# A fused decoder block on eight cores: three weight loads issued later, zero columns written once, the last 128 tokens in narrower column groups

## The chip, the cores and the metric

The program runs on the 8 cores of one Trainium2 chip. Each core works on one of the 8 sequences of the batch, with the same weights, and the cores do not exchange data. The metric is the time of one execution in microseconds of the device, taken on the slowest of the eight cores. "Before" is the kernel as it stood, "after" is the changed one.

## The reference

Each core computes one decoder block for a sequence of 2048 tokens with 1024 channels:

```
z = x @ w_in                                  # q, k, v | pool input | gates
y_attn = moba_attention(q, k, v) @ w_branch_attn
y_pool = multiscale_pool(u_pool) @ w_branch_pool
mix = (g_attn * y_attn + g_pool * y_pool) @ w_out
x = layer_norm(ALPHA * x + mix, ln1_g, ln1_b)
a = x @ w_ffn_gate                            # (2048, 2816)
u = x @ w_ffn_up
ap = pad(a, two zero tokens in front)
a = sum(ap[:, i:i + s] * conv_w[i] for i in range(3)) + conv_b
ffn = (gelu(a) * u) @ w_ffn_down
x = layer_norm(ALPHA * x + ffn, ln2_g, ln2_b)
```

The change touches three places: the gated merge (`mix`) with the loads around it, the two zero tokens ahead of the causal convolution, and the last product with the layer norm behind it.

## The kernel before, in words

The tokens are worked on in two halves of 1024. All tiles are placed by hand in one SBUF arena, and a small scheduler in the kernel (`Sched`) records every operation in program order, finds the overlaps of what is read and written, and puts a semaphore wait ahead of an operation where another engine, a DMA or an earlier operation of the same engine has to be done. Each engine runs its operations in the order in which they were recorded. The order on TensorE is made by `weave`, which takes pieces of generators (`Stream`) in turn by a virtual time; a load that a generator records between two of its `yield`s doesn't change that order.

There are two DMA queues. `ld_cast` (L407) issues loads on GpSimd's queue (POOL in the profile) that cast float32 in HBM to bf16 in SBUF: all weights. `ld`, `ld_x1` and the output writes are issued on SP's queue.

The stages, in order: projections and attention woven together; `merge(0)` at the end of that; then `merge(1)` woven with `oproj(0)` (output projection, first layer norm, transposes into `x1T`); then `p7_gen(0)` (gate and up products, convolution, GELU) woven with `oproj(1)`; then `p7_gen(0)` alone, `p8(0)` (down product and second layer norm), `p7_gen(1)`, `p8(1)`.

The merge of one half runs over 8 column blocks j. A block uses one of three buffers `wm` (L407, 768 KB of bf16 each), and behind a block `mg_load` issues the load of the block three further on into the buffer that has come free. The load that is issued behind block j = 0 of the second half is thus needed at block j = 3. `wout`, 2048 KB, is issued when the first weave is through, just ahead of the second half's merge, and `p7_load` three times right behind it: it loads the gate/up weights `wgu` of one f (a block of 128 of the 2816 channels, 512 KB) into one of three buffers. `p7_gen` uses one buffer for each f and issues the load of f + 3 behind it.

In `p7_gen` the gate product of 1024 tokens goes into `abuf[f % 2]`, a float32 row of two columns ahead of 1024. In the first half the two columns are zero (a memset on VectorE, L453), in the second half they are the last two columns of the first half, kept in `halo`.

In `p8` a tile of 128 tokens has two PSUM banks of 512 columns. For each, 22 matmuls of 128 x 512 are followed by a scalar_tensor_tensor that adds the residual (L449) and a bn_stats (L1120); then come bn_aggr (L1122), an addition of EPS (L441), a square root on ScalarE (L433), a reciprocal (L462), and for each half of the columns two scalar_tensor_tensor and a DMA to `out` (L1130). For the last tile all of that stands behind the last matmul of the program.

Of the kernel before, what the change touches and what calls it, by code (L numbers as in the profile page):

```python
# [6 lines left out]
F32 = mybir.dt.float32  # L7
BF16 = mybir.dt.bfloat16
U8 = mybir.dt.uint8
AF = mybir.ActivationFunctionType  # L10
# [8 lines left out]
NF = 22  # L19
# [251 lines left out]
def build_program():  # L271
# [32 lines left out]
    def T(name, shape, dt, off):  # L304
        n = 2 if dt == BF16 else 4
        for d in shape[1:]:
            n *= d
        assert off + n <= ARENA, name
        h = nc.alloc_sbuf_tensor_at(name, list(shape), dt, offset=abase + off)
        S.reg(h, "sb", abase + off, 256 * KB)  # L310
        return h
# [15 lines left out]
    mhalf = T("mhalf", [128, 1], F32, o); o += 32  # L327
    rs = T("rs", [128, 16], F32, o); o += 64
    ps0 = T("psc0", [128, 1], F32, o); o += 32
    assert o <= 4 * KB, o  # L330
    rcw = small[:, 0:16]
    bgate = small[:, 16:32]
# [52 lines left out]
    gbuf = [T(f"gbuf{i}", [128, 512], F32, 174 * KB + 8256 + (2 + i) * 2 * KB) for i in range(2)]  # L385
    assert 174 * KB + 8256 + 8 * KB <= 194 * KB
    wgu = [T(f"wgu{i}", [128, 2, 8, 128], BF16, (194 + 4 * i) * KB) for i in range(3)]

    ps = []
    for i in range(8):  # L390
# [15 lines left out]
    def ld_cast(dst, src, after=()):  # L406
        S.dma("pool", lambda e: e.dma_start(out=dst, in_=src), reads=list(after), writes=[dst])  # L407
# [44 lines left out]
    def memset(eng, ap, val):  # L452
        S.op(eng, lambda e: e.memset(ap, val), writes=[ap])  # L453
# [63 lines left out]
    ld_cast(kh[64:72, :, :], oh8)  # L517
    ld_cast(tri[:], tri_d)
    ld_cast(identb[:], ident_d)
    memset("dve", uh[:], 0.0)  # L520
    memset("pool", mhalf[:], -0.5)
    act(rs[:, 0:1], uh[:, 0, 0:1], AF.Copy)
# [372 lines left out]
    def mg_load():  # L895
        k = mg_n[0]
        mg_n[0] += 1
        if k < 16:
            ld_cast(wm[k % 3][:], wm_d[k % 8])

    def merge(half):
        ui = 0
        for j in range(8):
            w = (half * 8 + j) % 3
            for tl in range(2):
                x_ = xc[half * 2 + tl]
                cs = slice(tl * 512, (tl + 1) * 512)
                s = ui % 2
                ui += 1
                b2 = nbank()  # L910
                for dt in range(8):
                    mm(b2[:, :], wm[w][:, dt, :], x_[:, dt, :], dt == 0, dt == 7)
                    if dt % 4 == 3:
                        yield 4
                act(sga[s][:, :], b2[:, :], AF.Tanh, bias=hb[:, j:j + 1], scale=0.5)
                tile_end()
                b3 = nbank()
                for dt in range(8):
                    mm(b3[:, :], wm[w][:, 8 + dt, :], x_[:, dt, :], dt == 0, dt == 7)
                    if dt % 4 == 3:  # L920
                        yield 4
                act(sgp[s][:, :], b3[:, :], AF.Tanh, bias=hb[:, 8 + j:9 + j], scale=0.5)
                tile_end()
                b0 = nbank()
                for ct in range(4):
                    mm(b0[:, :], wm[w][:, 16 + ct, :], ATT[half][:, ct, cs], ct == 0, ct == 3)
                yield 4
                stt("dve", m1[s][:, :], sga[s][:, :], 1.0, b0[:, :], ALU.add, ALU.mult)
                b1 = nbank()
                for g in range(4):  # L930
                    mm(b1[:, :], wm[w][:, 20 + g, :], PL[half][:, g, cs], g == 0, g == 3)
                yield 4
                stt("dve", m2[s][:, :], sgp[s][:, :], 1.0, b1[:, :], ALU.add, ALU.mult)
                tt("pool", mix[half][:, j, cs], m1[s][:, :], m2[s][:, :], ALU.add)
            mg_load()


    def o_mm(T_):
# [92 lines left out]
    def p7_gen(half, xT):  # L1031
        ui = 0
        pend_tail = []

        def flush_tail():
            while pend_tail:
                s_, f_, cs_, bu_ = pend_tail.pop(0)
                act(gbuf[s_][:, :], cbuf[s_][:, :], AF.Gelu)
                tt("dve", hT[:, f_, cs_], gbuf[s_][:, :], bu_[:, :], ALU.mult)

        for f in range(NF):
            ab = abuf[f % 2]
            if half == 0:
                memset("dve", ab[:, 0:2], 0.0)
            else:
                cp("dve", ab[:, 0:2], halo[:, f, :])
            for c in range(2):
                cs = slice(c * 512, (c + 1) * 512)
                ba, bu = nbank(), nbank()
                w = wgu[(half * NF + f) % 3]  # L1050
                for k, bk in ((0, ba), (1, bu)):
                    for dt in range(8):
                        mm(bk[:, :], w[:, k, dt, :], xT[:, dt, cs], dt == 0, dt == 7)
                        if dt % 4 == 3:
                            yield 4
                s = ui % 2
                ui += 1
                act(ab[:, 2 + c * 512:2 + (c + 1) * 512], ba[:, :], AF.Copy)
                act(cbuf[s][:, :], ba[:, :], AF.Identity, bias=convb[:, f:f + 1], scale=convw[:, f, 2:3])
                stt("dve", cbuf[s][:, :], ab[:, 1 + c * 512:1 + (c + 1) * 512], convw[:, f, 1:2], cbuf[s][:, :], ALU.mult, ALU.add)  # L1060
                stt("dve", cbuf[s][:, :], ab[:, c * 512:(c + 1) * 512], convw[:, f, 0:1], cbuf[s][:, :], ALU.mult, ALU.add)
                flush_tail()
                pend_tail.append((s, f, cs, bu))
            if half == 0:
                cp("dve", halo[:, f, :], ab[:, 1024:1026])
            if half == 1 or f < NF - 3:
                p7_load()
            if half == 0 and f % 2 == 0 and f < 12:
                ld_cast(wd[0][:, f:min(f + 2, 11), :], wd_d[:, f:min(f + 2, 11), :])
            if half == 0 and not O1.live:  # L1070
                wd_late(1)
        flush_tail()
# [10 lines left out]
    def ld_x1(t_):  # L1083
        rw = row[t_ % 4]
        S.dma("sp", lambda e: e.dma_start(out=rw[:, :], in_=x1_d[t_ * 128:(t_ + 1) * 128, :]),
              reads=[("x1", t_)], writes=[rw[:, :]])

    def p8(half):
        banks = {}

        def dmm(tl, bk, hv, f):
            mm(bk[:, :], hT[:, f, tl * 128:(tl + 1) * 128], wd[f // 11][:, f % 11, hv * 512:(hv + 1) * 512], f == 0, f == NF - 1)

        for tl in range(8):
# [10 lines left out]
            if tl == 0:  # L1105
                n0 = 3 if half == 0 else 1
                for t2 in range(1, n0):
                    banks[t2] = [nbank(), nbank()]
                mid = 11 if half == 0 else NF - 1
                for t2 in range(n0):  # L1110
                    for hv in range(2):
                        for f in range(mid):
                            dmm(t2, (bks if t2 == 0 else banks[t2])[hv], hv, f)
            first = (11 if half == 0 else (NF - 1 if tl == 0 else 0)) if tl < (3 if half == 0 else 1) else 0
            for hv in range(2):
                for f in range(first, NF):
# [24 lines left out]
    ld(ln1b[:], lnp_d[1])  # L1141
    M1 = Stream(merge(1))
    O0 = Stream(oproj(0, 1.35), 120.0)
    for _ in range(3):
        p7_load()
    weave([M1, O0], [M1, O0])

    O1 = Stream(oproj(1, 3.3), 24.0)
# [97 lines left out]
```

How the kernel before makes its waits and increments, by code:

```python
        def run(engname, e):  # L220
            for o in per_eng.get(engname, []):
                for (sk, val) in o.waits:
                    e.wait_ge(semh(sk), val)
                inst = o.fn(e)
                if o.sig:
                    inst.then_inc(semh(o.sem), o.inc)
```

## Time and profile before

| | |
|---|---|
| Time before, median of 3 runs | 971.28 us (970.56 to 972.38) |
| The profiled execution's own time | 971.86 us |
| Its span on the slowest core (core 1) | 970.3 us |
| Spans of the eight cores | 965.2 to 970.3 us |
| TensorE (PE) busy, core 1 | 930.4 us, 96% of the span |
| VectorE (DVE) busy | 585.4 us, 60% |
| ScalarE (ACT) busy | 459.6 us, 47% |
| GpSimd (POOL) busy | 227.7 us, 23% |

The profile is of one execution. The own time is 1.56 us longer than the span of the slowest core, and 0.58 us above the median of the runs. Busy time of an engine is the union of its instructions; the chain of work tells what each piece waited for, and the timeline lists instructions with the idle time ahead of them in brackets.

### The profile page before, as it was taken

The numbers are of one execution on the slowest core, as the hardware profiler recorded it, in microseconds if no ns is written. First come the engines' busy times: TensorE is split into PE (matmuls) and PEld (weight loads), VectorE is DVE, ScalarE is ACT, GpSimd is POOL, SyncE is SP. The second block draws the span as 40 slices with busy tenths as digits, with TensorE's granted clock in tenths as the row PEclk, the third lists the DMA queues.
The fourth block names the chain that finished last, engine by engine and source line by source line (L and its number), as shares of the span: only waits on it lengthen the run. The fifth ranks groups of instructions, "written<-read, shape, count | busy, mean of one in ns | idle before, by whom it ended". The sixth has DMA issues, their size and how long they took to land.

```text
span 970.3 us, 16929 instructions; the slowest of 8 cores (965.2 to 970.3 us)
## 1 busy us (share of the span) xinstructions
PE 930.4 (96%) x4992; PEld 472.7 (49%) x4992; DVE 585.4 (60%) x1072; ACT 459.6 (47%) x839; POOL 227.7 (23%) x233
## 2 busy tenths in 40 slices
PE   4998998999999999999999999999999999999996
PEld 1444554666666654444444444444444444444442
DVE  6849754663433333556468787763777666665756
ACT  2365676777777741245544555660004555553000
POOL 5734644411111132445213231310000000000000
PEclk9999999999999999999999999999999999999999
DMA  8963200431213269562456655598325444540221
GB/s 134 188 129 57 55 1 25 88 67 36 56 34 77 45 130 158 149 162 76 130 111 152 140 110 109 107 217 144 131 87 156 84 81 73 83 70 1 105 90 66
DMA packets 30970, 94.95 MB, mean 98 GB/s; under 512 B 4880, under 2 KB 8336, under 8 KB 30240
## 3 DMA queue, kind: packets, MB, share of 16 engines
q0 software_dynamic: 12688, 52.70, 32.1%
q1 hardware_dynamic: 18192, 41.17, 13.2%
q8 instruction: 42, 0.69, 0.3%
q14 instruction: 48, 0.39, 0.1%
HBM read 125.11 MB, written 16.78 MB: 146 GB/s over the span
## 4 chain that ended last, share of the span: by engine, by line
PE 87%; DMA 5%; DVE 2%; issue 2%; POOL 1%; SPq 1%; ACT 1%; DVEq 0%; POOLq 0%; ACTq 0%
PE ps L416 87%; DMA wm<-wm 3%; DMA xT<-xT 1%; DMA q<-hst 1%; SPq L413 1%; PE ps L420 1%; POOL P L436 1%; DVE t L436 1%; DVE hT L436 0%; DVE row L449 0%; DVE PT L855 0%; ACT abuf L433 0%; POOL hst L436 0%; POOL mix L436 0%; DVE row L436 0%
## 5 line engine op out<-in xcount | busy, mean ns | idle before, releaser
L416 PE MATMUL ps<-x1T,wgu 128*128 128x512 bf16 x1408 | 310.9, 379 | 4.1 <-DVE hT L436 2.2
L416 PEld LDWEIGHTS ps<-x1T,wgu 128*128 128x128 bf16 x1408 | 137.2, 98 | 171.1 <-issue 8.1
L449 DVE SCALAR_TENSOR_TENSOR cbuf<-abuf,small,cbuf 128x512 f32<-128x512 f32 x176 | 145.5, 827 | 100.0 <-ACT cbuf L433 90.1
L433 ACT ACTIVATE PT<-ps 128x512 bf16<-128x512 f32 (+1 forms) x288 | 154.3, 573 | 85.0 <-PE ps L416 77.8
L416 PE MATMUL ps<-xT,wm 128*128 128x512 bf16 x512 | 127.1, 381 | 3.3 <-DMA wm<-wm 3.3
L416 PE MATMUL ps<-PT,Vp 128*128 128x256 bf16 (+1 forms) x584 | 106.0, 265 | 4.5 <-DVE PT L855 4.3
L416 PE MATMUL ps<-q,k 72*128 72x256 bf16 x576 | 106.9, 266 | 2.1 <-DMA q<-hst 1.9
L433 ACT ACTIVATE abuf<-ps 128x512 f32<-128x512 f32 x88 | 52.4, 596 | 109.8 <-PE ps L416 109.8
L407 POOL DMA_DIRECT2D wgu<-wgu x44 | 23.9, 542 | 293.3 <-PE ps L416 285.6
L436 POOL TENSOR_TENSOR mix<-m,m 128x512 bf16<-128x512 f32 x32 | 41.6, 1299 | 178.3 <-DVE m L449 174.0
L416 PE MATMUL ps<-wdb,hT 128*128 128x512 bf16 x352 | 80.4, 379 | 0.0
L416 PE MATMUL ps<-wda,hT 128*128 128x512 bf16 x352 | 80.4, 379 | 0.0
L416 PEld LDWEIGHTS ps<-q,k 72*128 72x128 bf16 x576 | 55.5, 98 | 48.7 <-issue 3.8
L416 PE MATMUL ps<-xT,wqk 128*128 128x512 bf16 x256 | 64.0, 394 | 14.1 <-DMA xT<-xT 14.1
L416 PEld LDWEIGHTS ps<-xT,wm 128*128 128x128 bf16 x512 | 49.3, 98 | 50.2 <-issue 4.9
L433 ACT ACTIVATE cbuf<-ps,small 128x512 f32<-128x512 f32 x88 | 68.3, 777 | 0.0
L416 PE MATMUL ps<-wout,mix 128*128 128x512 bf16 x256 | 66.6, 383 | 0.0
L433 ACT ACTIVATE lnmv<-lnmv 128x1 f32<-128x1 f32 x16 | 3.3, 204 | 127.5 <-DVE lnmv L441 127.5
L436 DVE TENSOR_TENSOR hT<-gbuf,ps 128x512 bf16<-128x512 f32 x88 | 59.9, 680 | 1.3 <-ACT gbuf L433 1.2
L416 PEld LDWEIGHTS ps<-PT,Vp 128*128 128x128 bf16 x584 | 53.1, 97 | 13.7 <-issue 6.9
L433 ACT ACTIVATE gbuf<-cbuf 128x512 f32<-128x512 f32 x88 | 55.6, 631 | 3.6 <-DVE cbuf L449 3.3
L416 PEld LDWEIGHTS ps<-wdb,hT 128*128 128x128 bf16 x352 | 34.4, 98 | 41.5
(107 smaller groups left out, 1034.9 us busy)
## 6 DMA issues: line engine op xcount, KB each, us to landing
wgu<-wgu POOLq DMA_DIRECT2D x44, 512.0 KB, 5.4
wm<-wm POOLq DMA_DIRECT2D x16, 768.0 KB, 8.2
xres<-x SPq DMA_DIRECT2D x16, 512.0 KB, 4.5
x1s<-row SPq DMA_DIRECT2D x16, 512.0 KB, 3.1
row<-x1s SPq DMA_DIRECT2D x16, 512.0 KB, 7.7
out<-row SPq DMA_DIRECT2D x32, 256.0 KB, 2.0
wda<-wd POOLq DMA_DIRECT2D x5, 512.0 KB, 7.6
wdb<-wd POOLq DMA_DIRECT2D x3, 768.0 KB, 21.3
```

The lines of the kernel that those rows point to most:

```text
L407: S.dma("pool", lambda e: e.dma_start(out=dst, in_=src), reads=list(after), writes=[dst])
L413: S.dma("sp", lambda e: e.dma_start(out=dst, in_=src), reads=[src], writes=[dst])
L416: S.op("pe", lambda e: e.matmul(out, lhsT, rhs, start=start, stop=stop), reads=[lhsT, rhs], writes=[out])
L420: S.op("pe", lambda e: e.transpose(out, in_, ident), reads=[in_, ident], writes=[out])
L433: S.op("act", lambda e: e.activation(out=out, in_=in_, func=func, **kw), reads=rd, writes=[out])
L436: S.op(eng, lambda e: e.tensor_tensor(out=out, in0=in0, in1=in1, op=op), reads=[in0, in1], writes=[out])
L449: S.op(eng, lambda e: e.scalar_tensor_tensor(out=out, in0=in0, scalar=scalar, in1=in1, op0=op0, op1=op1), reads=rd, writes=[out])
```

## The change

Three edits. The three `p7_load` calls that stood ahead of the weave of `merge(1)` and `oproj(0)` are gone, and `merge` of the second half calls `p7_load` once behind each of the blocks j = 3, 4 and 5, after the `mg_load` of that block. The memset of the two zero columns is recorded only for f = 0 and f = 1 of the first half, once for each of the two buffers; nothing else writes those columns until the second half. The last tile of the program goes through a new function, `last_tile`: its first 512 columns are one group, the other 512 are two groups of 256 in two banks, bn_stats runs on pieces of 256, EPS comes in as the bias of the square root instead of as an addition of its own, and the reciprocal is recorded behind the first of the last scalar_tensor_tensor.

```diff
@@ -327,6 +327,7 @@
     mhalf = T("mhalf", [128, 1], F32, o); o += 32
     rs = T("rs", [128, 16], F32, o); o += 64
     ps0 = T("psc0", [128, 1], F32, o); o += 32
+    epsb = T("epsb", [128, 1], F32, o); o += 32
     assert o <= 4 * KB, o
     rcw = small[:, 0:16]
     bgate = small[:, 16:32]
@@ -386,6 +387,8 @@
     assert 174 * KB + 8256 + 8 * KB <= 194 * KB
     wgu = [T(f"wgu{i}", [128, 2, 8, 128], BF16, (194 + 4 * i) * KB) for i in range(3)]
 
+    sfin = T("sfin", [128, 4, 6], F32, 0)
+
     ps = []
     for i in range(8):
         p = nc.alloc_psum_tensor(f"ps{i}", [128, 512], F32)
@@ -517,6 +520,7 @@
     ld_cast(kh[64:72, :, :], oh8)
     ld_cast(tri[:], tri_d)
     ld_cast(identb[:], ident_d)
+    memset("dve", epsb[:], EPS)
     memset("dve", uh[:], 0.0)
     memset("pool", mhalf[:], -0.5)
     act(rs[:, 0:1], uh[:, 0, 0:1], AF.Copy)
@@ -933,6 +937,8 @@
                 stt("dve", m2[s][:, :], sgp[s][:, :], 1.0, b1[:, :], ALU.add, ALU.mult)
                 tt("pool", mix[half][:, j, cs], m1[s][:, :], m2[s][:, :], ALU.add)
             mg_load()
+            if half == 1 and 3 <= j < 6:
+                p7_load()
 
 
     def o_mm(T_):
@@ -1040,9 +1046,9 @@
 
         for f in range(NF):
             ab = abuf[f % 2]
-            if half == 0:
+            if half == 0 and f < 2:
                 memset("dve", ab[:, 0:2], 0.0)
-            else:
+            if half == 1:
                 cp("dve", ab[:, 0:2], halo[:, f, :])
             for c in range(2):
                 cs = slice(c * 512, (c + 1) * 512)
@@ -1085,6 +1091,35 @@
         S.dma("sp", lambda e: e.dma_start(out=rw[:, :], in_=x1_d[t_ * 128:(t_ + 1) * 128, :]),
               reads=[("x1", t_)], writes=[rw[:, :]])
 
+    def bns(out, in_):
+        S.op("dve", lambda e: e.bn_stats(out=out, in_=in_), reads=[in_], writes=[out])
+
+    def out_dma(t_, rw, a, b, key):
+        S.dma("sp", lambda e: e.dma_start(out=out_d[t_ * 128:(t_ + 1) * 128, a:b], in_=rw[:, a:b]),
+              reads=[rw[:, a:b]], writes=[key])
+
+    def last_tile(t_, rw, mv, bks, dmm):
+        for f in range(NF):
+            dmm(7, bks[0], 0, f)
+        stt("dve", rw[:, 0:512], rw[:, 0:512], ALPHA, bks[0][:, :], ALU.mult, ALU.add)
+        bns(sfin[:, 0, :], rw[:, 0:256])
+        bns(sfin[:, 1, :], rw[:, 256:512])
+        for i, bk in ((2, bks[1]), (3, nbank())):
+            a, b = i * 256, (i + 1) * 256
+            for f in range(NF):
+                mm(bk[:, 0:256], hT[:, f, 896:1024], wd[f // 11][:, f % 11, a:b], f == 0, f == NF - 1)
+            stt("dve", rw[:, a:b], rw[:, a:b], ALPHA, bk[:, 0:256], ALU.mult, ALU.add)
+            bns(sfin[:, i, :], rw[:, a:b])
+        S.op("dve", lambda e: e.bn_aggr(out=mv[:, 0:2], in_=sfin[:].rearrange("p a b -> p (a b)")),
+             reads=[sfin[:]], writes=[mv[:, 0:2]])
+        act(mv[:, 2:3], mv[:, 1:2], AF.Sqrt, bias=epsb[:, 0:1])
+        for a in (0, 512):
+            stt("dve", rw[:, a:a + 512], rw[:, a:a + 512], mv[:, 0:1], ln2g[:, a:a + 512], ALU.subtract, ALU.mult)
+            if a == 0:
+                recip(mv[:, 2:3], mv[:, 2:3])
+            stt("dve", rw[:, a:a + 512], rw[:, a:a + 512], mv[:, 2:3], ln2b[:, a:a + 512], ALU.mult, ALU.add)
+            out_dma(t_, rw, a, a + 512, ("out", t_, a // 512))
+
     def p8(half):
         banks = {}
 
@@ -1111,6 +1146,9 @@
                     for hv in range(2):
                         for f in range(mid):
                             dmm(t2, (bks if t2 == 0 else banks[t2])[hv], hv, f)
+            if half == 1 and tl == 7:
+                last_tile(t_, rw, mv, bks, dmm)
+                continue
             first = (11 if half == 0 else (NF - 1 if tl == 0 else 0)) if tl < (3 if half == 0 else 1) else 0
             for hv in range(2):
                 for f in range(first, NF):
@@ -1141,8 +1179,6 @@
     ld(ln1b[:], lnp_d[1])
     M1 = Stream(merge(1))
     O0 = Stream(oproj(0, 1.35), 120.0)
-    for _ in range(3):
-        p7_load()
     weave([M1, O0], [M1, O0])
 
     O1 = Stream(oproj(1, 3.3), 24.0)
```

The first place is GpSimd's queue between the two halves of the merge. Below is what stands there before: `mix_117` is the merged tile of the second half, and the two rows with `mix_117` are its block j = 0.

```order
L407 DMA wm_119<-wm 128x3072
L407 DMA wout<-wout 128x8192
L407 DMA wgu_154<-wgu 128x2048
L407 DMA wgu_155<-wgu 128x2048
L407 DMA wgu_156<-wgu 128x2048
L436 TENSOR_TENSOR mix_117<-m_0_125,m_0_127 128x512
L436 TENSOR_TENSOR mix_117<-m_1_126,m_1_128 128x512
L407 DMA wm_120<-wm 128x3072
```

The same place in the changed kernel, where all lines and tile numbers are a few higher (`wm_121` is the third of the `wm` buffers, as `wm_120` is above):

```order
L410 DMA wm_120<-wm 128x3072
L410 DMA wout<-wout 128x8192
L439 TENSOR_TENSOR mix_118<-m_0_126,m_0_128 128x512
L439 TENSOR_TENSOR mix_118<-m_1_127,m_1_129 128x512
L410 DMA wm_121<-wm 128x3072
```

The three gate/up loads no longer stand between `wout` and the merge weights of block j = 3. They now stand further on; the following is GpSimd's order in the changed kernel from the end of block j = 3 to the end of block j = 4, between small operations of the layer norm of `oproj(0)` (`lnmv`, `row`):

```order
L439 TENSOR_TENSOR mix_118<-m_1_127,m_1_129 128x512
L410 DMA wm_121<-wm 128x3072
L410 DMA wgu_155<-wgu 128x2048
L439 TENSOR_TENSOR lnmv<-lnmv,mhalf 128x1
L439 TENSOR_TENSOR row_136<-row_136,ln1b 128x1024
L439 TENSOR_TENSOR mix_118<-m_0_126,m_0_128 128x512
L439 TENSOR_TENSOR lnmv<-lnmv,mhalf 128x1
L439 TENSOR_TENSOR row_137<-row_137,ln1b 128x1024
L439 TENSOR_TENSOR mix_118<-m_1_127,m_1_129 128x512
L410 DMA wm_119<-wm 128x3072
L410 DMA wgu_156<-wgu 128x2048
```

Each gate/up load stands behind a merge load, and the third one (`wgu_157`, not shown) behind the last row of block j = 5, where no merge load is left.

The other place is the end of the program on VectorE. Before, from the last tile's first sum with the residual on:

```order
L449 SCALAR_TENSOR_TENSOR row_136<-row_136,ps 128x512
L1120 BN_STATS lnst<-row_136 128x6
L449 SCALAR_TENSOR_TENSOR row_136<-row_136,ps 128x512
L1120 BN_STATS lnst<-row_136 128x6
L1122 BN_AGGR lnmv<-lnst 128x2
L441 TENSOR_SCALAR lnmv<-lnmv 128x1
L462 RECIPROCAL lnmv<-lnmv 128x1
L449 SCALAR_TENSOR_TENSOR row_136<-row_136,lnmv,ln2g 128x512
L449 SCALAR_TENSOR_TENSOR row_136<-row_136,lnmv,ln2b 128x512
L449 SCALAR_TENSOR_TENSOR row_136<-row_136,lnmv,ln2g 128x512
L449 SCALAR_TENSOR_TENSOR row_136<-row_136,lnmv,ln2b 128x512
```

The same in the changed kernel (`sfin` is the new tile of statistics):

```order
L452 SCALAR_TENSOR_TENSOR row_137<-row_137,ps 128x512
L1095 BN_STATS sfin<-row_137 128x6 x2
L452 SCALAR_TENSOR_TENSOR row_137<-row_137,ps 128x256
L1095 BN_STATS sfin<-row_137 128x6
L452 SCALAR_TENSOR_TENSOR row_137<-row_137,ps 128x256
L1095 BN_STATS sfin<-row_137 128x6
L1113 BN_AGGR lnmv<-sfin 128x2
L452 SCALAR_TENSOR_TENSOR row_137<-row_137,lnmv,ln2g 128x512
L465 RECIPROCAL lnmv<-lnmv 128x1
L452 SCALAR_TENSOR_TENSOR row_137<-row_137,lnmv,ln2b 128x512
L452 SCALAR_TENSOR_TENSOR row_137<-row_137,lnmv,ln2g 128x512
L452 SCALAR_TENSOR_TENSOR row_137<-row_137,lnmv,ln2b 128x512
```

The addition is gone, the reciprocal has moved one place back, and the sum and the statistics that stand last ahead of bn_aggr are on 256 columns.

## Rows read from the trace of the kernel before

**Rows 1.** The page: busy time, share of the span and instructions of each engine.
```profile
PE 930.4 (96%) x4992; PEld 472.7 (49%) x4992; DVE 585.4 (60%) x1072; ACT 459.6 (47%) x839; POOL 227.7 (23%) x233
```

**Rows 2.** Spans and granted clock of two of the cores.
```profile
core 1: 970.3 us, clock 0.995
...
core 4: 968.5 us, clock 0.996
```

**Rows 3.** Timeline of TensorE, core 1: start, duration, instruction, count, idle time before.
```profile
389.29 1.54 PE L416 MATMUL ps<-xT,wm 128*128 128x512 bf16 x4 [3.27 <-DMA wm<-wm]
...
394.43 1.03 PE L416 MATMUL ps<-wout,mix 128*128 128x512 bf16 x4
```

**Rows 4.** A stretch behind it: length, TensorE busy, granted clock, DMA share, GB/s.
```profile
390.60:392.30 1.70, 1.70 (x5) 0.50 0.88 196
```

**Rows 5.** The same place on core 4, timeline of TensorE.
```profile
389.32 1.02 PE L416 MATMUL ps<-xT,wm 128*128 128x512 bf16 x4 [2.92 <-DMA wm<-wm]
```

**Rows 6.** Timeline of GpSimd's queue, core 1, 351 to 364 us.
```profile
351.82 0.54 POOL L407 DMA_DIRECT2D wout<-wout  x1
...
353.95 1.06 POOL L407 DMA_DIRECT2D wgu<-wgu  x2 [1.07 <-DVE ATT L436]
...
363.13 0.58 POOL L407 DMA_DIRECT2D wm<-wm  x1
```

**Rows 7.** DMA issues in windows around 351.82 and 363.13: KB, us to landing.
```profile
wout<-wout POOLq DMA_DIRECT2D x1, 2048.0 KB, 22.8
...
wm<-wm POOLq DMA_DIRECT2D x1, 768.0 KB, 26.0
```

**Rows 8.** Timeline of GpSimd behind the merge load of block j = 3.
```profile
416.35 0.56 POOL L436 TENSOR_TENSOR lnmv<-lnmv,mhalf 128x1 f32<-128x1 f32 x1 [3.11 <-DVE lnmv L441]
```

**Rows 9.** Timeline of TensorE: the first gate/up matmuls; then all gate/up loads' landing.
```profile
469.66 5.56 PE L416 MATMUL ps<-x1T,wgu 128*128 128x512 bf16 x25
...
DMA to landing us min/median/max: 5.1/5.4/30.8
```

**Rows 10.** The memsets (duration min/median/max in ns); whom TensorE waited for.
```profile
L453 DVE MEMSET abuf<- x22: 60/60/60, 470.6 to 653.3; 128x2 f32 x22
...
PE ps L416 <- DVE hT L436: 2.2, 2, 1.8
```

**Rows 11.** Timeline of TensorE where matmuls of 512 and 256 columns follow each other.
```profile
300.05 1.02 PE L416 MATMUL ps<-xT,wm 128*128 128x512 bf16 x4
300.91 0.38 PE L416 MATMUL ps<-q,k 72*128 72x256 bf16 x2
301.13 0.38 PE L416 MATMUL ps<-PT,Vp 128*128 128x256 bf16 x2
```

**Rows 12.** VectorE by form: the one float32 group that reads 256 PSUM columns (busy, mean ns).
```profile
L645 DVE TENSOR_TENSOR gm<-ps,AM 128x256 f32<-128x256 f32 x2 | 0.8, 425 | 3.4 <-PE ps L416 3.3
```

**Rows 13.** Timeline of core 1's end, VectorE and ScalarE, from the last sum on.
```profile
962.22 0.69 DVE L449 SCALAR_TENSOR_TENSOR row<-row,ps 128x512 f32<-128x512 f32 x1 [2.44 <-PE ps L416]
...
963.80 0.21 DVE L1122 BATCH_NORM_AGGREGATE lnmv<-lnst 128x2 f32<-128x12 f32 x1
964.12 0.15 DVE L441 TENSOR_SCALAR lnmv<-lnmv 128x1 f32<-128x1 f32 x1
964.37 0.20 ACT L433 ACTIVATE lnmv<-lnmv 128x1 f32<-128x1 f32 x1 [9.29 <-DVE lnmv L441]
964.67 0.16 DVE L462 RECIPROCAL lnmv<-lnmv 128x1 f32<-128x1 f32 x1 [0.40 <-ACT lnmv L433]
964.75 0.73 DVE L449 SCALAR_TENSOR_TENSOR row<-row,lnmv,ln2g 128x512 f32<-128x512 f32 x1
965.60 0.75 DVE L449 SCALAR_TENSOR_TENSOR row<-row,lnmv,ln2b 128x512 f32<-128x512 f32 x1
966.27 0.75 DVE L449 SCALAR_TENSOR_TENSOR row<-row,lnmv,ln2g 128x512 f32<-128x512 f32 x1
967.12 0.75 DVE L449 SCALAR_TENSOR_TENSOR row<-row,lnmv,ln2b 128x512 f32<-128x512 f32 x1
```

## The prediction, as it stood before the changed kernel was run

> **What bounds the kernel now.** I read the page first, then the spans of the cores, the list of who TensorE waited for, the chain of work, and the timeline around each of TensorE's waits. TensorE is busy for 930.4 of 970.3 us [rows 1, 2], so only its idle time, its slow stretches and what stands behind its last matmul can give anything. Edits on other engines count only where they end one of its waits. The reader is to look for three things: a wait inside the run of matmuls, what that wait does to the granted clock, and the chain after the last matmul.
>
> The wait is at 386.0 us. The matmul of merge block j = 3 starts at 389.29, with 3.27 us of idle time ahead of it that a merge-weight DMA ended [rows 3]. Behind it the matmuls are slow: from 389.29 to 394.43 there are 16 matmuls of 512 columns (4, 4 and 8), which at the usual 0.215 us each [rows 11] would take 3.44 us. They take 5.14, so 1.70 us are lost in addition. The granted clock there is 0.50 [rows 4], the lower of the two levels, 1.2 GHz instead of 2.4, after an engine that had been busy without a break stood still. Core 4 has the same wait, 2.92 us, but its four matmuls behind it take 1.02 us, the same as four matmuls elsewhere: no slow stretch [rows 5, 11]. So the place costs 4.97 us on core 1 and 2.92 us on core 4.
>
> **The change, part one: the three loads.** GpSimd's queue takes `wout` at 351.82, the three gate/up loads by about 355 and the merge load for j = 3 at 363.13 [rows 6]. `wout` lands 22.8 us after its issue, at 374.6; the merge load lands 26.0 us after its issue, at 389.1 [rows 7]. In the 14.5 us between the two landings the three gate/up loads of 512 KB and the merge load of 768 KB go through, 2304 KB in all. The three are 1536 KB of these, two thirds, which is 9.7 us. Without them the merge load would land at about 379.4, and TensorE wants it at 386.0: a margin of 6.6 us. Loads of the queue seem to be served in the order of issue, since the merge load, issued when `wout` was halfway, took all that time. With the wait gone the slow stretch has nothing to start it.
>
> Here a rule of the Trainium skill speaks against so wide a margin. "DMA: Bandwidth & Descriptors", section "Anatomy of one DMA — SWDGE (gpsimd) path", gives a load from GpSimd about 2.0 us plus its bytes by 436 KB per us. By that the three loads would hold the queue for only 3.6 us (an estimate from that page), and the merge load would land at 385.5, a bare 0.5 us ahead of its need. The trace has 14.5 us for 2304 KB, less than half of the page's rate; by either figure the wait of core 1 is gone.
>
> What the loads cost at their new place: each is one issue of about 0.55 us on GpSimd [rows 6]. Behind the merge load of block j = 3, GpSimd waits 3.11 us for VectorE before its next operation [rows 8], so the issue is hidden; without that cover it would delay a layer norm piece of `oproj(0)` by 0.55 us. I take zero, and 3 x 0.55 = 1.7 us as the upper bound. What is late next: the weights of f = 0 are now issued at some 408 us on core 1: GpSimd's wait behind that merge load began at 413.24 (416.35 less 3.11), and everything here moves up by 5. They are needed at 469.66 less 5, 464.7 [rows 9]. The third load comes two blocks j later, with two more blocks of the merge still to run, and is wanted only at f = 2. A usual landing takes 5.4 us and the slowest of all took 30.8 [rows 9]: none is late. The merge loads of j = 4 to 7 gain as well, since the queue is shorter when they are issued.
>
> What that makes of the slowest core: core 1 goes from 970.3 to 970.3 - 4.97 = 965.3, core 4 from 968.5 to 968.5 - 2.92 = 965.6 [rows 2, 3, 5]. The other six come out below. So core 4 is the slowest then, and the slowest span falls by 970.3 - 965.6 = **4.7 us**.
>
> **Part two: the memsets.** Twenty memsets of 60 ns go [rows 10], one is added at the start for EPS. Once `oproj(1)` is through, TensorE doesn't wait any more, and there they cost nothing. Where `oproj(1)` runs beside `p7_gen(0)`, TensorE waits for VectorE's product into `hT`, 2.2 us in two waits [rows 10]. In the stretch in which VectorE is late, at most one or two memsets lie ahead of each. I take **0.1 us**. Nothing is the lower bound; the 20 together, 1.2 us, the upper.
>
> **Part three: the end.** (a) TensorE: 22 matmuls of 512 columns become 44 of 256. Two of 256 start 0.22 us apart from the next two, four of 512 take 0.86 us [rows 11]. So 44 x 0.110 = 4.84 us for 22 x 0.215 = 4.73: 0.1 us lost. The bound above is the full length of such a pair, 0.38 us, with nothing of it overlapped: 22 x 0.38 = 8.36, 3.6 us lost. I take the small one, since the rows have exactly these widths, each matmul with weights of its own. (b) The last sum and the last bn_stats are on 256 columns. From the sum's start to bn_aggr's they take 1.58 us, 0.79 each [rows 13]. A float32 operation that reads 256 PSUM columns takes 425 ns, the sum of 512 takes 690 [rows 12, 13]; for bn_stats I take the same saving, 0.26 us each, 0.52 together; bounds 0 and 0.7. The middle group and its statistics end while TensorE works on the last 22 matmuls of 2.4 us. (c) From bn_aggr's start to the end of the last operation it is 967.87 - 963.80 = 4.07 us [rows 13]. After: the first of the four can start where the addition started, 0.32 us in; square root and reciprocal fit into its 0.73 us (the root needs from 0.32 to 0.52, and the reciprocal starts 0.30 behind a root's start now). The reciprocal starts 0.67 behind the first (as 966.27 does behind 965.60), at 0.99; the second of the four 0.26 later (0.16 and a gap of 0.10, as between dependent operations here), at 1.25; the third at 1.92, the fourth at 2.77, the end at 3.52. That saves 0.55; bounds 0.3 and 0.7. Sum of part three: 0.52 + 0.55 - 0.1 = **1.0 us**, between 3.3 lost and 1.4 won.
>
> **The sum.** 4.7 + 0.1 + 1.0 = 5.8 us. The slowest span becomes 964.5 us. The profiled execution's own time of 971.86 lies 1.56 above its span, so its counterpart would be 966.1; the median of the runs shown is 0.58 below that execution, which gives 971.28 - 5.8 = **965.5 us**.
>
> **The rivals.**
> 1. *The clock didn't matter in most runs.* The slow stretch is on core 1, not on core 4, so whether the slowest core has one is chance. If the median run had none, only the wait goes: 2.9 + 1.1 = 4.0 us, 967.3. For it: core 4, at 968.5, is only 1.8 us below core 1 [rows 2]. Against it: the profiled execution, near the median, has one on its slowest core. 25%.
> 2. *The wait stays.* If the merge load had been held back by the sheer traffic and by `wout` rather than by the three loads in between, only 1.1 us would come: 970.2, no difference that can be told. For it: the DMA engines are busy at 0.88 even in rows 4, after the wait. Against it: the order of issue and the two landings [rows 6, 7]. 4%.
> 3. *Matmuls of 256 columns don't overlap with their weight loads at the end.* The bound of (a): 5.8 - 3.5 = 2.3 us won, 969.0. Against it: rows 11. 5%.
> 4. *On the other side: the gate/up weights come late.* GpSimd's queue is in order, and the three loads now stand behind merge operations that wait for VectorE, which waits for TensorE. If they were issued only at the end of the merge, near 464.7 us, and landed as slowly as the slowest, 30.8 us, `p7_gen(0)` would start 30.8 us late, 25 lost in all: 996. It decides from a landing 5.8 us behind the need, 470.5 us, on. Against it: the place of the loads in the order, some 57 us ahead of their need for the first. 2%.
>
> The forecast itself has 64%, and its own range is 964.3 to 966.6.
>
> **How the numbers follow.** A measurement of this kernel can tell about 0.2% from no change, 1.9 us here. The forecast, rival 1 and rival 3 lie beyond that: 0.64 + 0.25 + 0.05 = 0.94 faster. Rival 2 is the same, 0.04, and rival 4 slower, 0.02. The range is to hold 8 in 10. Above it reaches over rival 1 with the scatter of the runs, 967.3 + 0.7 = 968.0. Below it takes what core 1 alone would give, 5.0, with 0.5 for the memsets and 1.3 for the end, 6.8, to 964.5, and the same scatter, to 963.8. Rivals 2 to 4 stay outside.
>
> **What the changed profile would show.** Right: no idle time of TensorE that a merge weight ended; `wout` landing near its old 22.8 us after issue, and the merge load behind it in about 16 instead of 26.0; a granted clock of 1.00 from 380 to 400 us on all cores; three gate/up issues, the first near 408 us and the others one and two blocks later, without a wait for them on TensorE; the last 44 matmuls in about 4.8 us, and about 4.6 us instead of 5.65 from the start of the last sum to the end of the last operation. Wrong: a new wait of TensorE for `wout` or a merge load, for `x1b` or `hT` between 375 and 642 us, or a slow stretch elsewhere on the slowest core that wasn't there before.

## The result and the profile after

The changed kernel takes 966.26 us (median of 5 runs, 964.75 to 967.27), the kernel before 970.93 us in the same series (5 runs, 969.28 to 972.38). The ratio is 0.9942 with a 95% interval of 0.993 to 0.9955: 0.6% faster, a gain of 4.4 to 6.8 us by the interval. Forecast were 965.5 us and a range of 963.8 to 968.0. A few executions in which one die ran at a much lower clock are left out of all times and ratios. The medians differ by 4.7 us; the gain by the ratio, 0.0058 x 970.93, is 5.6 us.

The page and the spans of the cores after; the chain of work is shown by engine:

```profile
span 964.7 us, 16930 instructions; the slowest of 8 cores (961.0 to 964.7 us)
...
PE 931.1 (97%) x5014; PEld 475.5 (49%) x5014; DVE 586.1 (61%) x1055; ACT 459.1 (48%) x839; POOL 227.5 (24%) x233
...
PE 92%; DVE 3%; issue 2%; DMA 1%; ACT 1%; POOL 1%; DVEq 0%; ACTq 0%; POOLq 0%
```

The slowest span fell from 970.3 [rows 2] to 964.7 us, but it is another core now, core 6. It has a slow stretch at 90 to 150 us, where the edits change nothing, that no other core of the two traces has there:

```profile
90.00:120.00 30.00, 28.09 (x177) 0.96 0.17 48
120.00:150.00 30.00, 29.91 (x183) 0.98 0.01 3
```

A granted clock of 0.96 and 0.98 in two stretches of 30 us means 3.6 us at half speed (0.04 and 0.02 of 30 us, each doubled), an estimated 1.8 us lost. On core 1 the span went from 970.3 to 962.2 us, and TensorE's busy time from 930.4 [rows 1] to 928.3: matmuls at half speed count as busy, so the end of a slow stretch shows there, and the rest of what went is idle time and the end. Part of these 8.1 us is chance, too: TensorE's waits for the first `xT` are 14.1 us in the one trace and 11.9 in the other.

**The merge weights.** Who TensorE waited for on the slowest core (us in total, times, longest), all five entries of that list, then GpSimd's queue (its timeline), then two answers on DMA issues around 352 and 363 us (us to landing last), and a stretch of TensorE (length, busy, granted clock, DMA share, GB/s), all on core 6:

```profile
PE ps L419 <- DMA xT<-xT: 13.9, 2, 12.6
PE ps L419 <- DVE PT L859: 4.3, 6, 1.4
PE ps L419 <- DVE t L439: 3.5, 2, 2.5
PE ps L419 <- DVE hT L439: 2.1, 3, 1.5
PE ps L419 <- DVE halo L459: 1.6, 2, 1.1
```

```profile
363.43 0.57 POOL L410 DMA_DIRECT2D wm<-wm  x1
...
408.41 0.54 POOL L410 DMA_DIRECT2D wgu<-wgu  x1
411.53 0.56 POOL L439 TENSOR_TENSOR lnmv<-lnmv,mhalf 128x1 f32<-128x1 f32 x1 [2.58 <-DVE lnmv L444]
```

```profile
wout<-wout POOLq DMA_DIRECT2D x1, 2048.0 KB, 23.7
...
wm<-wm POOLq DMA_DIRECT2D x1, 768.0 KB, 17.4
```

```profile
380.00:400.00 20.00, 20.00 (x95) 1.00 0.52 120
```

No merge weight ends a wait any more, here or on any other core (in [rows 3, 5] it was 3.27 and 2.92 us). `wout` lands after 23.7 us, near its old 22.8. The merge load lands 17.4 us after its issue, at 380.8, 5.4 us ahead of the first matmul that needs it (386.16 in the timeline). The 26.0 us of [rows 7] are those of another core; the median of the eight cores was 25.75 us and is 16.7 now. The clock stays at its upper level through the stretch in which [rows 4] had 0.50. The first gate/up load is issued at 408.41, and GpSimd still waits 2.58 us for VectorE behind it, in place of 3.11 us [rows 8]: the issue lies in that wait.

**The end.** The last 11 matmuls of TensorE and VectorE's and ScalarE's operations behind them, to be held against [rows 13]:

```profile
955.62 1.36 PE L419 MATMUL ps<-wdb,hT 128*128 128x256 bf16 x11
957.44 0.42 DVE L452 SCALAR_TENSOR_TENSOR row<-row,ps 128x256 f32<-128x256 f32 x1 [1.79 <-PE ps L419]
957.97 0.43 DVE L1095 BATCH_NORM_STATS2 sfin<-row 128x6 f32<-128x256 f32 x1
958.50 0.26 DVE L1113 BATCH_NORM_AGGREGATE lnmv<-sfin 128x2 f32<-128x24 f32 x1
958.86 0.29 ACT L436 ACTIVATE lnmv<-lnmv,epsb 128x1 f32<-128x1 f32 x1 [8.96 <-DVE lnmv L1113]
958.88 0.75 DVE L452 SCALAR_TENSOR_TENSOR row<-row,lnmv,ln2g 128x512 f32<-128x512 f32 x1
959.54 0.16 DVE L465 RECIPROCAL lnmv<-lnmv 128x1 f32<-128x1 f32 x1
959.82 0.75 DVE L452 SCALAR_TENSOR_TENSOR row<-row,lnmv,ln2b 128x512 f32<-128x512 f32 x1
960.48 0.74 DVE L452 SCALAR_TENSOR_TENSOR row<-row,lnmv,ln2g 128x512 f32<-128x512 f32 x1
...
961.33 0.75 DVE L452 SCALAR_TENSOR_TENSOR row<-row,lnmv,ln2b 128x512 f32<-128x512 f32 x1
```

From the start of the last sum to the end of the last operation it is 962.08 - 957.44 = 4.64 us, where it was 5.65. The sum takes 0.42 and not 0.69 us, bn_stats 0.43, the addition is gone, and the reciprocal fits between the first and the second of the four last operations. But something else is to be seen: TensorE's last matmul ends at 955.62 + 1.36 = 956.98, and VectorE starts only 0.46 us later. Before, the last 11 matmuls started at 959.56 and took 2.54 us, to 962.10, and VectorE started at 962.22, 0.12 later. That is 0.34 us lost, on all eight cores alike. The section on the hardware comes back to it.

### The profile page after: what moved, and what is told of

Same layout as the page of the kernel before. It is cut to its first block, busy times and chain, and to the rows that moved or that the text cites. A ratio compares the mean times of both kernels' runs of the same rounds, so it can differ in the third digit from the quotient of the medians.

```text
span 964.7 us, 16930 instructions; the slowest of 8 cores (961.0 to 964.7 us)
## 1 busy us (share of the span) xinstructions
PE 931.1 (97%) x5014; PEld 475.5 (49%) x5014; DVE 586.1 (61%) x1055; ACT 459.1 (48%) x839; POOL 227.5 (24%) x233
## 4 chain that ended last, share of the span: by engine, by line
PE 92%; DVE 3%; issue 2%; DMA 1%; ACT 1%; POOL 1%; DVEq 0%; ACTq 0%; POOLq 0%
PE ps L419 91%; DMA xT<-xT 1%; PE ps L423 1%; POOL P L439 1%; DVE hT L439 0%; DVE t L439 0%; ACT cbuf L436 0%; DVE row L452 0%; DVE cbuf L452 0%; DVE PT L859 0%; ACT abuf L436 0%; DVE row L439 0%; ACT PT L436 0%; ACT gbuf L436 0%; DVE PLt L452 0%
## 5 line engine op out<-in xcount | busy, mean ns | idle before, releaser
L419 PE MATMUL ps<-wdb,hT 128*128 128x512 bf16 (+1 forms) x363 | 80.6, 373 | 0.0
L419 PE MATMUL ps<-wda,hT 128*128 128x512 bf16 (+1 forms) x363 | 80.6, 373 | 0.0
L419 PEld LDWEIGHTS ps<-wda,hT 128*128 128x128 bf16 x363 | 35.5, 98 | 40.7
```

What stands on the lines that cost most here:

```text
L419: S.op("pe", lambda e: e.matmul(out, lhsT, rhs, start=start, stop=stop), reads=[lhsT, rhs], writes=[out])
```

## The experiments

Times are medians, ratios are to the kernel before on the same chip. The first four kernels shared one chip, the next four another, the last ones a third. Landing times of the merge load of block j = 3 are compared by their median over the eight cores (25.75 us before), since they differ by about 1 us from core to core.

**1. One edit at a time.** Each kernel is the one before with one of the three edits of the diff, as it stands there.

The loads alone:

> The kernel before with the first edit alone: the three gate/up loads behind blocks j = 3, 4 and 5 of the second merge. Theory (the three loads hold the merge load of block j = 3 back): TensorE has no wait for a merge weight on any core, the granted clock is 1.00 there, and the time falls by 3.5 to 4.7 us, the larger part of the whole gain. Rival (the wait comes from wout and the traffic as such): the wait of 2 to 3 us stays and the time doesn't change.

Measured: 967.47 us against 972.04, ratio 0.995 (0.9937 to 0.9963). No core waits for a merge weight; the granted clock there is 1.00 on all of them, and the merge load lands after 16.1 us. 4.6 us of the whole gain are in this edit, between 3.6 and 6.1 by the interval. That it is the order of the loads and not the traffic as such, this version can't tell, since the three loads have left the place altogether; experiment 3 can.

The zero columns alone:

> The kernel before with the second edit alone: the zero columns are written for f = 0 and 1 only. Theory: 0 to 0.3 us faster, nothing that can be told from no change; TensorE's waits for the product into hT while oproj(1) runs get at most 0.1 us shorter each. Rival (a memset stands in the way of the convolution each time): 20 memsets of 0.06 us with their semaphore waits are worth 1.2 us or more.

Measured: 971.85 us against 972.04, ratio 0.9999 (0.9989 to 1.001). In the time it is nothing. In the trace there is a cleaner measure: the start of the first and of the last gate/up matmul on core 1, both inside a stretch in which every clock is 1.00. Before, with this edit alone, and after:

```profile
L416 PE MATMUL ps<-x1T,wgu x1408: 376/379/379, 469.7 to 885.7; 128*128 128x512 bf16 x176
```

```profile
L416 PE MATMUL ps<-x1T,wgu x1408: 376/379/379, 468.8 to 884.5; 128*128 128x512 bf16 x176
```

```profile
L419 PE MATMUL ps<-x1T,wgu x1408: 376/379/379, 462.5 to 878.1; 128*128 128x512 bf16 x176
```

That is 416.0, 415.7 and 415.6 us: the memsets were worth 0.3 to 0.4 us, not 1.2. The five other cores that this view shows in full agree within 0.2 us.

The end alone:

> The kernel before with the third edit alone: the last 128 tokens in groups of 512, 256 and 256 columns, with EPS as the bias of the square root and the reciprocal one place later. Theory: 1.0 us faster; in the profile 4.6 us instead of 5.65 from the start of the last sum to the end of the last operation of VectorE, and 44 matmuls in 4.84 us instead of 22 in 4.73. Rival (256 columns don't overlap with their weight loads): the 44 matmuls take up to 8.4 us and the time rises by up to 2.6 us.

Measured: 970.65 us against 972.04, ratio 0.9984 (0.9974 to 0.9993). The slowest core's end:

```profile
959.97 1.36 PE L419 MATMUL ps<-wdb,hT 128*128 128x256 bf16 x11
...
961.45 0.42 DVE L452 SCALAR_TENSOR_TENSOR row<-row,ps 128x256 f32<-128x256 f32 x1 [1.44 <-PE ps L419]
```

Here VectorE follows 0.12 us behind TensorE, with the same instructions that follow 0.46 behind in the changed kernel. The four runs of 11 matmuls start at 956.37, 957.57, 958.77 and 959.97, 1.20 us apart, so 44 take 4.80 us. From 956.37 to the end of the last operation it is 966.08 - 956.37 = 9.71 us. Before, from the start of the last 22 matmuls of 512 columns, which are the same work, it is 967.87 - 957.19 = 10.68. The end alone gives 0.97 us in the trace. The 44 matmuls are not held up by their weight loads: they start 0.109 us apart, the 22 wider ones 0.215.

**2. How long a load holds the queue.** One of the three loads is moved, two stay:

```diff
-    for _ in range(3):
+    for _ in range(2):
         p7_load()
     weave([M1, O0], [M1, O0])
...
             mg_load()
+            if half == 1 and j == 3:
+                p7_load()
```

> The kernel before, but only one of the three gate/up loads is moved behind block j = 3; two stay right behind wout. It tells how long one such load holds the queue. Theory (the trace's rate, 2304 KB in 14.5 us, so 3.2 us for 512 KB): the merge load lands 3.2 us earlier and TensorE's wait of 2.1 to 3.3 us shrinks to 0 to 0.1 us on every core; nearly the whole gain of the first edit, 3.5 to 4.6 us, is there. Rival (436 KB per us, so 1.2 us): the wait shrinks to 0.9 to 2.1 us, and only 1.2 us and what the clock gives come.

Measured: 966.92 us against 972.04, ratio 0.995 (0.9937 to 0.9963): as much as with all three. The landing of the merge load on the slowest core, core 5, and the only wait that is left, on core 3:

```profile
wm<-wm POOLq DMA_DIRECT2D x1, 768.0 KB, 22.4
```

```profile
385.77 1.02 PE L416 MATMUL ps<-xT,wm 128*128 128x512 bf16 x4 [0.20 <-DMA wm<-wm]
```

The median of the eight cores is 22.35 instead of 25.75: 3.4 us for 512 KB, near the 3.2 from the rate in the trace. At 436 KB per us, the rival, 0.9 us or more of wait would be left; seven cores have none.

Then the other way: two more loads of 512 KB ahead of the merge load, into space that is free.

```diff
+    for k_ in range(2):
+        ld_cast(xtra[k_][:], wgu_d[k_ + 3])
     for _ in range(3):
         p7_load()
```

> The kernel before with two more loads of 512 KB between wout and the merge load of block j = 3, into space that is free by then; nobody reads them. Theory (loads of this queue are served in the order of issue at 159 KB per us while it is full): 1024 KB more hold the merge load back by another 6.4 us, so TensorE waits about 9.5 us on core 1 instead of 3.3, the clock is at its lower level behind it on every core, and the time rises by 6.4 to 8 us. Rival (436 KB per us): the wait grows by 2.3 us, the time by 2.3 to 4. Rival (traffic ahead in the queue doesn't matter): no change.

Measured: 981.26 us against 972.59, ratio 1.0087 (1.0072 to 1.0102), 8.7 us slower by the medians, somewhat more than the 8 expected at most. Core 1, the slowest: its wait, the clock inside and behind it, and the landing of the merge load:

```profile
398.86 1.87 PE L418 MATMUL ps<-xT,wm 128*128 128x512 bf16 x4 [11.38 <-DMA wm<-wm]
```

```profile
389.00:391.00 2.00, 0.00 (x0) 1.00 1.06 171
391.00:393.00 2.00, 0.00 (x0) 0.68 1.04 224
393.00:398.80 5.80, 0.00 (x0) 0.50 1.04 200
398.80:402.50 3.70, 3.64 (x10) 0.57 0.99 184
402.50:406.00 3.50, 3.50 (x18) 1.00 0.86 178
```

```profile
wm<-wm POOLq DMA_DIRECT2D x1, 768.0 KB, 34.1
```

On core 1 the merge load lands 34.1 - 26.0 = 8.1 us later for 1024 KB, by the medians of the eight cores 7.85 (33.6 instead of 25.75), 3.9 for each load, somewhat more than the 3.2 expected. The waits are 10.0 to 11.4 us on the eight cores. The clock's fall can be seen here in full: TensorE stops at 387.5, the level falls inside the window from 391 to 393, and the first ten matmuls or so behind the wait run at half speed (four take 1.87 us instead of 1.02). On every core the first four take 1.86 or 1.87, while in the kernel before three cores had the slow stretch (after waits of 2.7, 3.0 and 3.3 us) and five had not (2.1 to 3.3 us). The rival of the fast queue, 2.3 us of wait more, falls.

**3. Does it matter where the loads go?** All three together, right behind the first merge load; the calls ahead of the weave are gone:

```diff
             mg_load()
+            if half == 1 and j == 0:
+                for _ in range(3):
+                    p7_load()
```

> The kernel before with all three gate/up loads issued together behind the first merge load of the second half (that of block j = 3), instead of one each behind the loads of j = 3, 4 and 5. Theory: the merge load of j = 3 is first in the queue and lands in time, so TensorE doesn't wait for it; the three loads then stand ahead of the merge load of j = 4, which is wanted some 14 us later than that of j = 3, and its landing moves to about 395, as before, so it is in time as well. The time is that of the first edit alone, 3.5 to 4.7 us below before. Rival (the wait is only handed on): TensorE waits for the merge load of j = 4 instead.

Measured: 966.76 us against 972.59, ratio 0.9936 (0.9922 to 0.9951). On core 7, the slowest, the loads around the first merge load, and TensorE from 380 to 400 us (length, busy, granted clock, DMA share, GB/s):

```profile
wgu<-wgu POOLq DMA_DIRECT2D x3, 512.0 KB, 21.6
wm<-wm POOLq DMA_DIRECT2D x1, 768.0 KB, 16.1
...
380.00:400.00 20.00, 20.00 (x94) 1.00 1.01 197
```

The merge load of j = 3 lands after 16.1 us, that of j = 4 after 21.0, at 395.6; no core waits for either. Here the three loads are in flight in the same stretch as in the kernel before, with the DMA engines at least as busy as before (a share of 1.01 against 0.93 in the same 20 us of core 1), and the merge load ahead of them lands as early as without them (median 16.35 us against 16.1 with the loads moved away). So it was their place ahead of the merge load and not the traffic; spreading them over j = 3 to 5 isn't needed.

**4. The end, taken apart.** The changed kernel with its old small operations:

```diff
-        act(mv[:, 2:3], mv[:, 1:2], AF.Sqrt, bias=epsb[:, 0:1])
+        ts("dve", mv[:, 1:2], mv[:, 1:2], EPS, None, ALU.add)
+        act(mv[:, 2:3], mv[:, 1:2], AF.Sqrt)
+        recip(mv[:, 2:3], mv[:, 2:3])
```

> The changed kernel with the old small operations at the end: EPS by an addition, the reciprocal ahead of the four last operations; the groups of 256 columns stay. Theory: 0.5 to 0.6 us slower than the changed kernel, so about 4.2 us faster than before, and 4.07 us from bn_aggr to the end. Rival (the order of the small operations is worth nothing): no difference from the changed kernel.

Measured: 966.22 us against 972.59, ratio 0.9933 (0.9918 to 0.9948). The changed kernel itself did not run on this chip, so the difference of half a microsecond can't be had from the time. From the last sum to the last operation's end it is 5.17 us on every core, against 4.64 in the changed kernel: 0.53 us for the small operations.

The changed kernel with one last group of 512 columns:

```diff
-        for i, bk in ((2, bks[1]), (3, nbank())):
-            a, b = i * 256, (i + 1) * 256
...
+        for f in range(NF):
+            dmm(7, bks[1], 1, f)
+        stt("dve", rw[:, 512:1024], rw[:, 512:1024], ALPHA, bks[1][:, :], ALU.mult, ALU.add)
+        bns(sfin[:, 2, :], rw[:, 512:768])
+        bns(sfin[:, 3, :], rw[:, 768:1024])
```

> The changed kernel with one group of 512 columns as the last one (22 matmuls, one sum), and bn_stats on two pieces of 256 behind it. Theory: the last matmul ends 0.1 us earlier, but the sum takes 0.69 instead of 0.42 us and two bn_stats of 256 follow instead of one, so the end is 0.5 us later; about 4.2 us faster than before. Rival (narrow matmuls cost as much as they give): no difference from the changed kernel.

Measured: 966.26 us against 972.59, ratio 0.9933 (0.992 to 0.9946). From the last sum to the end it is 5.23 us, 0.59 more than with 256 columns, and VectorE follows TensorE by 0.11 us here, not by 0.46. The two nearly cancel within 0.2 us, so in this kernel the narrow groups give next to nothing, and the rival comes near the truth for a reason of its own. In the version with the end alone, where the late start is missing, they are worth about 0.4 us: 0.97 in all less the 0.53 of the small operations.

**5. What might still be had.** The groups made finer still, 512, 256, 128 and 128, with bn_stats on pieces of 128:

```diff
+        for a, n, bk in ((512, 256, bks[1]), (768, 128, nbank()), (896, 128, nbank())):
+            b = a + n
...
+            for c in range(a, b, 128):
+                bns(sfin[:, c // 128, :], rw[:, c:c + 128])
```

> The changed kernel with the last 128 tokens in groups of 512, 256, 128 and 128 columns and bn_stats on pieces of 128. Theory: the last sum and bn_stats take about 0.29 us each instead of 0.42, TensorE loses another 0.05 us, bn_aggr over 48 instead of 24 elements takes 0.1 us more: 0.1 us faster in the profile of the end, nothing in the time. Rival (the step pays again as the one from 512 to 256 did, 0.5 us): 0.5 us faster.

Measured: 965.74 us against 972.33, ratio 0.9935 (0.992 to 0.995). From the last sum to the end it is 4.48 us, 0.16 less than in the changed kernel, and that sum starts 0.11 us behind TensorE and not 0.46; the time can't tell. bn_aggr takes 0.37 us over 48 elements.

The two halo columns of the first half copied by ScalarE:

```diff
-                cp("dve", halo[:, f, :], ab[:, 1024:1026])
+                act(halo[:, f, :], ab[:, 1024:1026], AF.Copy)
```

> The changed kernel, but in the first half ScalarE instead of VectorE copies the two halo columns (22 copies of 0.16 us on VectorE). It asks what small operations of VectorE are worth at all in that stage, in which the memsets of 0.06 us went. Theory (they count only where TensorE waits for VectorE, some one or two of them for each of five waits of 3.7 us in all): 0.2 to 0.5 us off these waits, 0.3 us faster at most, not to be told from the changed kernel. Rival (they count everywhere): 3.5 us faster than the changed kernel.

Measured: 964.83 us against 972.33, ratio 0.9923 (0.9906 to 0.994). It is the fastest version here that computes the right result, by its median and its ratio, though its interval overlaps that of the changed kernel. The gate/up stretch from the first to the last matmul is 415.0 us on core 1, 0.6 less than in the changed kernel, and VectorE's late start at the end is gone, too (0.11 us). TensorE's waits for VectorE in that stage are 3.2 us in five instead of 3.6 in five on core 1. How much of the 0.6 us comes from the copies themselves and how much from VectorE's instructions standing elsewhere in its stream, no run separates. The rival of 3.5 us falls.

The second output projection spread thinner, with a price of 3.6 for its pieces in the weave instead of 3.3:

```diff
-    O1 = Stream(oproj(1, 3.3), 24.0)
+    O1 = Stream(oproj(1, 3.6), 24.0)
```

> The same with a price of 3.6. By the density: again somewhat less waiting than with 3.5. Rival: the projection's last pieces come so late that TensorE has no gate/up matmuls left to put between them and waits for the layer norm chain, 1 to 3 us slower.

Measured: 965.77 us against 972.33, ratio 0.9937 (0.992 to 0.9953), no difference from the changed kernel. TensorE's waits for VectorE there are 3.3 us in four instead of 3.6 in five, on core 1: neither the gain of the density nor the loss of the rival. The same with a price of 3.5 took 964.37 us, but its result was wrong by a relative error of 0.049, for a reason that no run shows, so that time is not drawn on, and the question of density has one run only.

## Why the prediction came out right

- **The three loads held the merge load back.** Right, and the main term. Forecast was that the slowest span falls by 4.7 us; the edit alone gives 4.6. Taking away one load, taking away three and adding two moved the median landing by -3.4, -9.65 and +7.85 us, and three loads right behind the merge load left it at 16.35 us. So the queue serves in order, at 3.2 to 3.9 us for each 512 KB. The forecast of 9.7 us for the three is met by the loads alone; in the whole change it was 9.05, and the margin on core 6 was 5.4 us instead of the 6.6 forecast for core 1.
- **The rate of the rule.** The estimate by the Trainium skill's page "DMA: Bandwidth & Descriptors", 3.6 us for the three loads together, is what one of them took here. By it the version with one load moved would still wait, and seven of its cores don't; the measurement decides. All these KB are of the bf16 that is written. Counted by the float32 that they read it is twice as much, 4608 KB in the prediction's 14.5 us, or 318 KB per us. How much of what is still missing comes from eight cores loading at once, no run here shows.
- **The slow stretch behind the wait.** Right: it goes with the wait. That it comes by chance is right as well: three of eight cores had it, and eight of eight when the wait was over 10 us. The length of the wait doesn't decide it: a core with 2.7 us had one, and two with 3.2 and 3.3 had none. Rival 1, that only the wait counts in the median run, has 2.9 us for the loads alone, and their interval begins at 3.6.
- **The slowest core.** Forecast was 964.5 us on core 4; measured are 964.7 on core 6, which has a slow stretch of its own at 90 to 150 us. A slow stretch elsewhere on the slowest core was named as a sign of being wrong. It shows that the sum over single cores was too exact: the agreement within 0.2 us is luck, and the slowest spans of the five executions reach from 963.2 to 965.7.
- **The new place of the loads.** Right: the first at 408.41 (forecast near 408), hidden in a wait of GpSimd, and the weights in time.
- **The memsets.** The mechanism was right, the size too small: 0.3 to 0.4 us against 0.1. They counted somewhat more often than the two waits that I looked at. The list of the kernel before has two more in that stage on core 1, which ended on VectorE behind a memset:

```profile
PE ps L416 <- DVE abuf L453: 1.7, 2, 1.1
```

- **The end.** Its terms were right one by one: 44 matmuls in 4.80 us (4.84), 4.64 us from the last sum on (4.58), 0.97 in all with the edit alone (1.0). What was missing in my sum is the late start of the last sum, which takes 0.34 us of it back in the changed kernel.
- **The sum.** 4.6 + 0.35 + 0.97 - 0.34 = 5.6 us by these measurements, 5.8 forecast, 5.6 by the ratio, 4.7 by the medians. The interval of 4.4 to 6.8 us holds them all, so that the sum meets the ratio to the tenth is luck; the time itself, 966.26, is 0.8 above the forecast. The rivals of a wait that stays, of weight loads in the way and of late gate/up weights did not come.

## What to carry to other kernels

A queue of loads is a list of deadlines: look at each transfer for when it is wanted, and not only at which engine is idle. A load that is wanted 110 us later stood ahead of one wanted in 20, and moving a single one of the three was enough. The place to look is the landing time of a transfer that is long against its usual one (26.0 us against 8.2 for the same size), at a point where TensorE waits for it. A wait of a few microseconds in a long run of matmuls can cost more than its length, since the clock may fall behind it. And small savings on a side engine (20 memsets, 22 copies) count only by the few that stand ahead of a wait.

## What the runs showed of the hardware that was not expected

VectorE loses about 0.35 us at certain places of its instruction stream, and which operation is hit changes with the number of instructions ahead of it. In the changed kernel it is the start of the last sum, 0.46 us behind TensorE on all eight cores. In the version with the memsets gone and nothing else it is the addition of EPS at the end, which waits for nothing but the operation just ahead of it on the same engine:

```profile
962.86 0.21 DVE L1122 BATCH_NORM_AGGREGATE lnmv<-lnst 128x2 f32<-128x12 f32 x1
963.53 0.15 DVE L441 TENSOR_SCALAR lnmv<-lnmv 128x1 f32<-128x1 f32 x1 [0.46 <-DVE lnmv L1122]
```

The two starts are 0.67 us apart; in [rows 13] the same two are 0.32 apart. In the version with the finest groups it is a bn_stats behind its own sum:

```profile
956.42 0.49 DVE L1095 BATCH_NORM_STATS2 sfin<-row 128x6 f32<-128x128 f32 x2 [0.47 <-DVE row L452]
```

The traces themselves, each wait of VectorE counted as a row, say where these operations stand. In the changed kernel, in the one with its old small operations, in the one with the memsets gone alone and in the one with the finest groups, the late one is row 2236, on all eight cores. Row 2108 of the changed kernel, 128 rows earlier, is late as well. On core 6 it starts 0.39 us behind the start of the reciprocal ahead of it, where the same pair has 0.08 in [rows 13]; "issue" says that it waited for nothing that the profile shows:

```profile
902.52 0.16 DVE L465 RECIPROCAL lnmv<-lnmv 128x1 f32<-128x1 f32 x1 [0.40 <-ACT lnmv L436]
902.91 0.75 DVE L452 SCALAR_TENSOR_TENSOR row<-row,lnmv,ln2g 128x512 f32<-128x512 f32 x1 [0.23 <-issue]
```

And the DMA records have a queue for instructions. Between 957 and 960 us on core 6 of the changed kernel it moved one packet, at 958.10, 0.66 us behind the late start:

```profile
q14 instruction: 1, 0.01, 0.8%
```

It is a load of 8 KB. In all 32 core traces of these four kernels such a load begins 0.63 to 0.94 us behind the start of row 2236, and in the changed kernel one begins 0.65 to 0.9 us behind row 2108. In the other kernels it begins there too, from 0.15 us ahead of row 2236 to 1.2 behind it, but nothing waits for that row: before, it is a wait behind the first sum of the last tile but one; with one wide last group it is the wait ahead of bn_aggr, while a bn_stats still runs; with a price of 3.6, one row fewer stands ahead of the end, the row is the wait behind the last sum, and the sum starts 0.11 us behind TensorE. With the halo copies gone VectorE has 2230 rows in all; no such load comes in its last 50 us, and the last sum isn't late. So the late operation stands where a block of 128 rows of VectorE's instruction stream ends and a load of instructions follows. What takes the 0.34 us there stays open.

In the time, the edit of the memsets loses at the end what it gives in the middle: from the last sum on it has 6.00 us on all eight cores instead of 5.65, and 0.3 us less in the gate/up stretch, which agrees with its ratio of 0.9999. Which operation is hit is luck as far as the prediction goes: it counted no instructions.
